# Small tiles of a key selection: flip, count and level moved from SBUF to a PSUM bank

## The chip, the cores and the metric

The kernel runs on one core of one Trainium2 chip. The metric is the device time of one execution in microseconds. A core has TensorE (PE, matrix products), VectorE (DVE), ScalarE (ACT), GpSimd (POOL) and SyncE (SP, which issues the DMAs). SBUF is the working memory on the chip. PSUM holds what TensorE writes, in banks of 2 KB per partition; VectorE and ScalarE can read and write it too.

## The reference

One inference step of two layers over a prompt of 1024 tokens and 64 sample tokens (8 sequences of 8), width 1024. Layer 0 is attention with sparse heads and dilated window heads behind one input projection; layer 1 is a recurrent block; each has an MLP behind it. What matters here is the start of layer 0:

```
h = einsum('btd,de->bte', rmsnorm(x), w_in)          # queries, keys, values, index queries, index keys, index weights
sc = sum over h of wi[q, h] * relu(qi[q, h] . ki[s])  # index scores, query by key
sc = where(key <= query, sc, NEG)
_, idx = top_k(sc, 256)                               # each query attends to its 256 best keys
```

The kernel needs no order of the 256 keys, only a mask of the chosen ones. For a row of scores it finds the 256th largest value bit by bit and then sets to NEG whatever lies below it. The outputs are the two activations, the new key/value rows and the recurrent states.

## The kernel before

The work runs in stages with a barrier of all engines between them: the projections with the key selection (stage_project), window attention, sparse attention, sample attention, output projection, MLP, recurrent block, MLP. The change touches the first stage alone.

**Projections.** The input projection is cut into eight groups of columns (`GROUPS`): kikv, qi, qa, qk0, qk1, qk2, v01 and v2, numbered 0 to 7. Each group is computed for nine tiles of tokens: tile 0 holds the 64 sample tokens, tiles 1 to 8 hold 128 prompt tokens each. A full tile of a group takes 24 matmuls (L845: eight slices of 128 input columns, each as high by high, high by low and low by high part); tile 0 takes 16. Tile p writes PSUM bank p % 3 and waits until ScalarE has copied tile p - 3 out (L775, into `rows`). The copied rows are squared on ScalarE (L797), summed per head and scaled on VectorE (L1024, L1029), rooted on ScalarE (L720), inverted and applied on VectorE one tile later (L1036, L1040), multiplied by the gains on GpSimd (L652) and stored by SP (L549). `rows` has three buffers, so a copy also waits for the store of the tile three before it. Tile 0 of a group needs an addition on GpSimd (L645) before it is squared.

**Weights.** SP loads a group's weights in eight parts into three buffers. VectorE casts a part to its high half (L993) and GpSimd subtracts to make the low half (L617). `WEIGHTS_AT` spreads the parts of group g + 1 over the tiles of group g - 1 and g (two tiles per three parts, beginning on the last tile of the group before). The parts stand first in VectorE's step, except on the last tile of a group, where they stand behind the normalisation.

**Selection.** Six tiles of prompt queries (2 to 7, rows of 384 to 1024 scores) need a selection; the scores lie in SBUF as `select_work`. It runs beside groups 2 to 7, tile by tile (`STEPS`, 54 of them), in 32 rounds y = 0 to 31, one for each bit of the bound:

- Two of the six (`OWN_TILES`) are tried by VectorE itself: `try_own` counts the scores at or above the bound with two instructions (L250), `move_own` turns the sign of the count into a bit (L269) and puts it into the bound (L271). The rounds are spread over 43 steps. In a step they stand around the normalisation: `try_own`, norms, `move_own`.
- The other four are tried by ScalarE: `show` runs four activations of 640 to 1024 scores with Sign and an accumulated sum of signs (L292), into `signs`. It waits (`tried`) for the bound of the round before. On VectorE `turn` adds `level` to `signs` to give `count` (L303), makes the bit (L310) and puts it into `minus` (L312; round 0 has L307 in place of these two). Round y is shown in step 1 + 4y/3, behind that tile's copy, square and root, and turned first in the next step, behind that step's weight parts.

Each of these operations on counts and bounds covers 2 or 4 elements per partition. All their tiles (`count`, `flip`, `level`, `signs`, `bound`, `minus`) are in SBUF. After round 31 `settle` and then `close` (24 slices in all, four of them for each of the six query tiles; those of the two own tiles come before) turn the bounds into masks on VectorE (L322 to L359). The stage ends when all engines are through; the first matmul of the window stage is L1657.

**The bank.** `psx` (turn_ps) is a PSUM bank of 512 columns, used for sums of squares, transposes of keys and queries and the mixed sample scores. Its last use in this stage is VectorE's copy of the sample scores to `sample_work`, ahead of `topk_sample()` and of the selection's rounds.

Of the kernel before, what the change touches and what calls it, by code (L numbers as in the profile page):

```python
# [10 lines left out]
I32 = mybir.dt.int32  # L11
ALU = mybir.AluOpType
# [4 lines left out]
P = 128  # L17
# [104 lines left out]
NSEL = len(SEL_TILES)  # L122
# [3 lines left out]
OWN_TILES = 2  # L126
# [73 lines left out]
class Handover:  # L200


    def __init__(self, nc, ctx):
        self.all = ctx.enter_context(nc.sbuf_tensor("unit_raw", [P, 2, KD * P], F32))
        self.flat = self.all[:, :, :].rearrange("p u n -> p (u n)")
        self.rows = self.flat[:, 0:2 * 3 * BW].rearrange("p (s n) -> p s n", s=2)
        self.rows_in = [ctx.enter_context(nc.semaphore(f"sw_first_in{i}")) for i in range(2)]
        self.unit_in = [ctx.enter_context(nc.semaphore(f"d_w_in{i}")) for i in range(2)]


class Select:
# [4 lines left out]
    def __init__(self, nc, ctx, work):  # L216
        def sb(name, shape, dt=F32):
            return ctx.enter_context(nc.sbuf_tensor("select_" + name, shape, dt))

        def sem(name):  # L220
            return ctx.enter_context(nc.semaphore("select_" + name))

        self.nc, self.work = nc, work
        self.junk = self.tied = self.shown = None
        self.count = sb("count", [P, NSEL])
        self.room = sb("room", [P, NSEL])
        self.flip = sb("flip", [P, NSEL], I32)
        self.bound = sb("bound", [P, NSEL], I32)
        self.signs = sb("signs", [P, NSEL - OWN_TILES])
        self.level = sb("level", [P, NSEL - OWN_TILES])  # L230
        self.minus = sb("minus_bound", [P, NSEL - OWN_TILES], I32)
        self.keep = sb("keep", [P, NSEL - OWN_TILES])
        self.done, self.ready, self.signed, self.tried = (sem(n) for n in ("done", "ready", "signed", "tried"))
        self.n = self.closed = 0
# [24 lines left out]
    def move_own(self, dve, y):  # L259

        nc = self.nc
        part = slice(0, OWN_TILES)
        dve.wait_ge(self.done, self.n)
        said = self.count[:, part].bitcast(I32)
        if y == 0:
            self.mark(nc.vector.tensor_scalar(self.bound[:, part], said, 31, 1 << 30, ALU.arith_shift_right, ALU.bitwise_xor))
        else:
            b = BITS - y
            self.mark(nc.vector.tensor_scalar(self.flip[:, part], said, 31, b, ALU.logical_shift_right, ALU.logical_shift_left))  # L269
            dve.wait_ge(self.done, self.n)  # L270
            self.mark(nc.vector.scalar_tensor_tensor(out=self.bound[:, part], in0=self.flip[:, part], scalar=1 << (b - 1) if b else 0,  # L271
                                                     in1=self.bound[:, part], op0=ALU.bitwise_xor, op1=ALU.bitwise_xor))

    def prepare(self, pool):
# [9 lines left out]
    def show(self, act, y):  # L284

        act.wait_ge(self.tried, self.PREPARED + y)
        for x in range(OWN_TILES, NSEL):
            c = x - OWN_TILES
            v = self.scores(x)
            if y or c:  # L290
                act.wait_ge(self.signed, (NSEL - OWN_TILES) * y + c)
            self.nc.scalar.activation(self.shown[:, 0:v.shape[1]], v, ACT.Sign, bias=self.minus[:, c:c + 1].bitcast(F32),  # L292
                                      accum_out=self.signs[:, c:c + 1]).then_inc(self.signed, 1)

    def turn(self, dve, y):

        nc = self.nc
        part = slice(OWN_TILES, NSEL)
        dve.wait_ge(self.signed, (NSEL - OWN_TILES) * (y + 1))
        dve.wait_ge(self.tried, self.PREPARED + y)  # L300
        if y:
            dve.wait_ge(self.done, self.n)
        self.mark(nc.vector.tensor_tensor(self.count[:, part], self.signs[:, :], self.level[:, :], ALU.add))  # L303
        dve.wait_ge(self.done, self.n)
        said = self.count[:, part].bitcast(I32)
        if y == 0:
            nc.vector.tensor_scalar(self.minus[:, :], said, 31, -(1 << 30), ALU.arith_shift_right, ALU.bitwise_xor).then_inc(self.tried, 1)  # L307
            return
        b = BITS - y
        self.mark(nc.vector.tensor_scalar(self.flip[:, part], said, 31, b, ALU.logical_shift_right, ALU.logical_shift_left))  # L310
        dve.wait_ge(self.done, self.n)
        nc.vector.scalar_tensor_tensor(out=self.minus[:, :], in0=self.flip[:, part], scalar=1 << (b - 1) if b else 0,  # L312
                                       in1=self.minus[:, :], op0=ALU.bitwise_xor, op1=ALU.bitwise_xor).then_inc(self.tried, 1)

    def settle(self, dve):
# [47 lines left out]
def stage_project(nc, a, xh, xl, rstd, ident, work, sel, proj, kiwi, smask, table, halves, strips, wstrips, hand):  # L363
# [7 lines left out]
    with ExitStack() as ctx:  # L371
# [50 lines left out]
        psx = ctx.enter_context(nc.psum_tensor("turn_ps", [P, 512], F32))  # L422
# [405 lines left out]
        def _(pe):  # L828
# [56 lines left out]
            def project_with_scores(gi, i, j, turn):  # L885
                for pair in range(IH // 2):
                    score_pair(j, pair)
                    if pair == 2 and turn is not None:
                        turn_queries(turn)
                    project(gi, i, pair, IH // 2)  # L890
# [87 lines left out]
        def _(dve):  # L978
            tk = [0]

            def link(ins):

                tk[0] += 1
                ins.then_inc(S["topk"], 1)
                dve.wait_ge(S["topk"], tk[0])
# [56 lines left out]
            def topk_sample():  # L1042
                for r in range(SR):
                    link(nc.vector.max(m8[0:TS, :], wks[:, 0:SKEYS]))
                    link(nc.vector.match_replace(wks[:, 0:SKEYS], m8[0:TS, :], wks[:, 0:SKEYS], SENT))
                if SREST:
                    link(nc.vector.max(m8[0:TS, :], wks[:, :]))
                    link(nc.vector.match_replace(wks[:, :], m8[0:TS, :], wks[:, :], SENT))
                link(nc.vector.tensor_scalar(wks[:, 0:SKEYS], wks[:, 0:SKEYS], SENT, NEG, ALU.not_equal, ALU.mult))
# [47 lines left out]
            nc.vector.tensor_tensor(wks[:, PAST:SKEYS], wks[:, PAST:SKEYS], after[:, :], ALU.add).then_inc(S["s_taken"], 1)  # L1097
            dve.wait_ge(S["s_taken"], 2)
            topk_sample()

            before, r0 = None, 0
            parts = [("own", y) for y in range(BITS + 1)] + [("close", x, z) for x in range(OWN_TILES) for z in range(sel.SLICES)]
# [740 lines left out]
def stage_sample(nc, a, ident, work, smp, proj, obp, mixed, oas, obs, own, hand):  # L1843
# [6 lines left out]
    with ExitStack() as ctx:  # L1850
# [189 lines left out]
        def _(pe):  # L2040
# [7 lines left out]
            def turn_group(g):  # L2048
                turn(2 + g, [768 * (g + 1) + P * i for i in range(4)])
# [1451 lines left out]
```

## Time and profile before

| | us |
|---|---|
| three runs | 2664.79, 2650.52, 2659.28; median 2659.28 |
| profiled execution, its own time | 2656.01 |
| its span, first to last instruction | 2653.1 |
| TensorE busy over the span | 2542.2 (96%) |
| VectorE, ScalarE, GpSimd busy | 1567.5, 1049.5, 1242.8 |
| mean granted clock of TensorE, as a share | 0.976 |

The rows further down come from the one profiled execution. Times in them are microseconds from the start of the span; "L310" is line 310 of the kernel. A duration that is longer than the same instruction takes elsewhere holds time in which the instruction was started and could not proceed.

### The profile page before, as it was taken

To read this page: it belongs to the slowest core of one execution; us is meant where nothing else is said; L and a number is where in the kernel's file an instruction comes from. 1 tells how busy PE (TensorE), PEld (TensorE's weight loads), DVE (VectorE), ACT (ScalarE), POOL (GpSimd) and SP (SyncE) were. 2 spreads that over 40 slices of the span, in tenths; PEclk is the share of its full clock that TensorE was granted. 3 is DMA by queue.
4 is the path that set the end of the run, shared out by engine and by line. 5 is a ranking of instruction groups with operands and counts; after the bars stand their busy time and mean duration, and the time that the engine had idled before them with its cause. 6 is when DMAs were issued, how large, how long until landed. Compare 5 with 4: busy or idle time off the path is not lost.

```text
span 2653.1 us, 44709 instructions
## 1 busy us (share of the span) xinstructions
PE 2542.2 (96%) x16674; PEld 2354.5 (89%) x16674; DVE 1567.5 (59%) x2510; ACT 1049.5 (40%) x1883; POOL 1242.8 (47%) x833
## 2 busy tenths in 40 slices
PE   7899999889879999999999989998999999999998
PEld 6567778766659999999999979998999999999998
DVE  6269897436555555545655687566355545554557
ACT  5347785766532322232233242535232233223322
POOL 4114441007436555555466573323355466545655
PEclk9989999889989999999999999999999999999999
DMA  5402222634371111111111112223111111111112
GB/s 149 135 24 72 78 80 87 214 99 133 106 259 62 40 52 50 34 47 55 42 45 47 48 32 69 88 112 141 42 40 56 40 40 55 47 40 47 55 48 84
DMA packets 109203, 198.71 MB, mean 75 GB/s; under 512 B 22709, under 2 KB 62773, under 8 KB 108805
## 3 DMA queue, kind: packets, MB, share of 16 engines
q1 hardware_dynamic: 104602, 191.85, 22.9%
q10 hardware_dynamic: 4480, 5.27, 0.6%
q8 instruction: 73, 1.20, 0.2%
q14 instruction: 48, 0.39, 0.0%
HBM read 170.97 MB, written 47.17 MB: 82 GB/s over the span
## 4 chain that ended last, share of the span: by engine, by line
PE 66%; DVE 3%; issue 1%; ACT 1%; POOL 0%; DMA 0%; DVEq 0%; ACTq 0%
PE d_ps L2348 40%; PE d_ps L2875 24%; PE d_ps L3237 1%; PE d_ps L2363 1%; DVE rstd_all L2435 0%; DVE x_t L2979 0%; DVE x_t L2970 0%; DVE xg_low L3365 0%; DVE xg_low L2374 0%; DVE m_hidden L2923 0%; PE d_ps L2408 0%; DVE m_shared_part L2970 0%; DVE unit_high L2331 0%; POOL unit_low L2335 0%; DMA mixed_low<-mixed_t 0%
## 5 line engine op out<-in xcount | busy, mean ns | idle before, releaser
L2348 PE MATMUL d_ps<-xg_high,unit_high 128*128 128x364 f32 (+1 forms) x2112 | 472.0, 332 | 8.1 <-DVE xg_low L3365 2.1
L2348 PE MATMUL d_ps<-xg_high,unit_low 128*128 128x364 f32 (+1 forms) x2112 | 464.7, 329 | 0.0
L2348 PE MATMUL d_ps<-xg_low,unit_high 128*128 128x364 f32 (+1 forms) x2112 | 464.3, 328 | 0.0
L2335 POOL TENSOR_TENSOR unit_low<-unit_raw,unit_high 128x1024 fp32r<-128x1024 f32 x96 | 232.5, 2422 | 410.6 <-DVE unit_high L2331 229.5
L2875 PE MATMUL d_ps<-m_hidden_high,unit_high 128*128 128x272 f32 x1792 | 374.8, 291 | 14.0 <-DVE x_t L2970 8.9
L2348 PEld LDWEIGHTS d_ps<-xg_high,unit_high 128*128 128x128 f32 x2112 | 365.1, 188 | 14.5 <-issue 5.5
L2875 PE MATMUL d_ps<-m_hidden_high,unit_low 128*128 128x272 f32 x1792 | 371.9, 289 | 0.0
L2875 PE MATMUL d_ps<-m_hidden_low,unit_high 128*128 128x272 f32 x1792 | 371.6, 289 | 0.0
L2348 PEld LDWEIGHTS d_ps<-xg_high,unit_low 128*128 128x128 f32 x2112 | 366.7, 189 | 0.0
L2348 PEld LDWEIGHTS d_ps<-xg_low,unit_high 128*128 128x128 f32 x2112 | 365.0, 188 | 0.0
L2725 POOL TENSOR_TENSOR unit_low<-unit_raw,unit_high 128x512 fp32r<-128x512 f32 x128 | 176.5, 1379 | 392.3 <-ACT unit_high L2793 390.9
L2970 DVE TENSOR_TENSOR x_t<-x_t,d_ps 128x544 f32<-128x544 f32 x320 | 227.4, 718 | 134.7 <-PE d_ps L2875 134.2
L2793 ACT ACTIVATE unit_high<-unit_raw 128x512 fp32r<-128x512 f32 x128 | 81.1, 634 | 568.8 <-PE d_ps L2875 353.6
L2875 PEld LDWEIGHTS d_ps<-m_hidden_high,unit_high 128*128 128x128 f32 x1792 | 282.4, 189 | 15.6 <-issue 15.4
L2875 PEld LDWEIGHTS d_ps<-m_hidden_high,unit_low 128*128 128x128 f32 x1792 | 284.4, 190 | 0.0
L2875 PEld LDWEIGHTS d_ps<-m_hidden_low,unit_high 128*128 128x128 f32 x1792 | 281.5, 189 | 0.0
L2718 POOL TENSOR_TENSOR m_hidden_low<-m_hidden,m_hidden_high 128x544 fp32r<-128x544 f32 x160 | 250.8, 1591 | 23.1 <-ACT m_hidden_high L2782 23.1
L2923 DVE SCALAR_TENSOR_TENSOR m_hidden<-d_ps,rstd_all 128x1092 f32<-128x1092 f32 x64 | 82.5, 1292 | 293.8 <-PE d_ps L2348 293.7
L845 PE MATMUL proj_ps<-w_high,x_high 128*128 128x512 f32 (+2 forms) x464 | 181.4, 391 | 10.8 <-ACT rows L775 10.7
L845 PE MATMUL proj_ps<-w_low,x_high 128*128 128x512 f32 (+2 forms) x464 | 176.8, 381 | 0.0
L845 PE MATMUL proj_ps<-w_high,x_low 128*128 128x512 f32 (+2 forms) x464 | 176.8, 381 | 0.0
L2787 ACT ACTIVATE unit_high<-unit_raw 128x1024 fp32r<-128x1024 f32 x60 | 63.6, 1060 | 250.5 <-PE d_ps L2875 127.2
(401 smaller groups left out, 4188.6 us busy)
## 6 DMA issues: line engine op xcount, KB each, us to landing
unit_raw<-w_units SPq DMA_DIRECT2D x160, 512.0 KB, 3.6
unit_raw<-w_in SPq DMA_DIRECT2D x48, 256.0 KB, 2.9
proj_rows<-rows SPq DMA_DIRECT2D x32, 256.0 KB, 2.0
s_win<-win_cache SPq DMA_DIRECT2D x2, 3968.0 KB
proj_rows<-rows SPq DMA_DIRECT2D x36, 128.0 KB, 1.8
sw_rows<-proj_rows SPq DMA_DIRECT2D x12, 384.0 KB, 5.2
select_work<-xt SPq DMA_DIRECT2D x8, 546.0 KB, 4.0
x_t<-xt SPq DMA_DIRECT2D x4, 1092.0 KB, 14.2
```

Of the source, the lines that this page charges most:

```text
L845: last = nc.tensor.matmul(ps[p % 3][:, 0:w], x, y[gi % 2][:, k, 0:w], start=(n == 0), stop=(n == len(passes) - 1))
L2335: self.nc.gpsimd.tensor_tensor(self.wl[slot][:, :], self.raw[:, slot, :], self.wh[slot][:, :].bitcast(F32), ALU.subtract).then_inc(self.w_ ...
L2348: last = self.nc.tensor.matmul(ps[:, c, 0:USED[c]], w[wslot][:, wk], v[:, k, c, 0:USED[c]], start=(k == 0 and n == 0), stop=(k == nk - 1 a ...
L2363: last = self.nc.tensor.matmul(ps[:, c, 0:USED[c]], w[wslot][:, wk], v[:, k, c, 0:USED[c]], start=(k == 0 and n == 0), stop=(k == nk - 1 a ...
L2718: nc.gpsimd.tensor_tensor(hl[:, i, q, :], SOURCES[i], hh[:, i, q, :].bitcast(F32), ALU.subtract).then_inc(h_low, 1)
L2725: nc.gpsimd.tensor_tensor(out, src, top.bitcast(F32), ALU.subtract).then_inc(part_low, 1)
L2787: nc.scalar.activation(d.wh[slot], d.raw[:, slot, :], ACT.Copy).then_inc(d.w_high, 1)
L2793: nc.scalar.activation(part_slots(d.high, x), src, ACT.Copy).then_inc(part_high, 1)
L2875: last = nc.tensor.matmul(out[:, c, :], w[:, i // 4, c0:c0 + P], h[:, i, q, HC * c:HC * (c + 1)], start=(i < 4 and q == 0 and x == 0), sto ...
L2923: nc.vector.scalar_tensor_tensor(out=v[:, t, :].rearrange("p (c n) -> p c n", c=NCH), in0=d.ps[t][:, :, 0:CH], scalar=0.0, in1=d.rstd[:, : ...
L2970: nc.vector.tensor_tensor(out, out, d.quarter[i], ALU.add).then_inc(added, 1)
L3237: last = nc.tensor.matmul(ps[use % 2][:, c, 0:CC], gw[:, n % 2, x, :], cv[:, n % 2, c, :], start=True, stop=True)
```

## The change

`flip` goes from SBUF to the bank `psx`: columns 0 to 1 for the own tiles, 2 to 5 for the four others. In `turn`, `count` (columns 8 to 11) and `level` (columns 12 to 15) are in the bank too. A new function `place`, called once ahead of the rounds, copies `level` there. `signs`, `minus`, `bound` and the own tiles' `count` stay in SBUF, and `settle` and `close` are as they were. `turn` now waits for `done` in round 0 as well. The SBUF tile `flip` is gone.

```diff
@@ Select.__init__
-        self.junk = self.tied = self.shown = None
+        self.junk = self.tied = self.shown = self.bank = None
-        self.flip = sb("flip", [P, NSEL], I32)
@@ move_own
             b = BITS - y
-            self.mark(nc.vector.tensor_scalar(self.flip[:, part], said, 31, b, ALU.logical_shift_right, ALU.logical_shift_left))
+            flip = self.bank[:, 0:OWN_TILES].bitcast(I32)
+            self.mark(nc.vector.tensor_scalar(flip, said, 31, b, ALU.logical_shift_right, ALU.logical_shift_left))
             dve.wait_ge(self.done, self.n)
-            self.mark(nc.vector.scalar_tensor_tensor(out=self.bound[:, part], in0=self.flip[:, part], scalar=1 << (b - 1) if b else 0,
+            self.mark(nc.vector.scalar_tensor_tensor(out=self.bound[:, part], in0=flip, scalar=1 << (b - 1) if b else 0,
                                                      in1=self.bound[:, part], op0=ALU.bitwise_xor, op1=ALU.bitwise_xor))
@@ new, ahead of turn
+    def place(self, dve, bank):
+
+        self.bank = bank
+        dve.wait_ge(self.tried, self.PREPARED)
+        self.mark(self.nc.vector.tensor_copy(bank[:, 2 * NSEL:2 * NSEL + NSEL - OWN_TILES], self.level[:, :]))
+
@@ turn
-        part = slice(OWN_TILES, NSEL)
+        level = self.bank[:, 2 * NSEL:2 * NSEL + NSEL - OWN_TILES]
+        count, flip = self.bank[:, NSEL + OWN_TILES:2 * NSEL], self.bank[:, OWN_TILES:NSEL].bitcast(I32)
         dve.wait_ge(self.signed, (NSEL - OWN_TILES) * (y + 1))
         dve.wait_ge(self.tried, self.PREPARED + y)
-        if y:
-            dve.wait_ge(self.done, self.n)
-        self.mark(nc.vector.tensor_tensor(self.count[:, part], self.signs[:, :], self.level[:, :], ALU.add))
         dve.wait_ge(self.done, self.n)
-        said = self.count[:, part].bitcast(I32)
+        self.mark(nc.vector.tensor_tensor(count, self.signs[:, :], level, ALU.add))
+        dve.wait_ge(self.done, self.n)
+        said = count.bitcast(I32)
...
-        self.mark(nc.vector.tensor_scalar(self.flip[:, part], said, 31, b, ALU.logical_shift_right, ALU.logical_shift_left))
+        self.mark(nc.vector.tensor_scalar(flip, said, 31, b, ALU.logical_shift_right, ALU.logical_shift_left))
         dve.wait_ge(self.done, self.n)
-        nc.vector.scalar_tensor_tensor(out=self.minus[:, :], in0=self.flip[:, part], scalar=1 << (b - 1) if b else 0,
+        nc.vector.scalar_tensor_tensor(out=self.minus[:, :], in0=flip, scalar=1 << (b - 1) if b else 0,
                                        in1=self.minus[:, :], op0=ALU.bitwise_xor, op1=ALU.bitwise_xor).then_inc(self.tried, 1)
@@ stage_project, vector
             topk_sample()
+            sel.place(dve, psx)
```

## Rows read from the trace of the kernel before

**Rows 1.** Engines by stretch: us, busy (instructions) per engine, PE clock, DMA share, GB/s.
```profile
203.00:437.00 234.00, 224.20 (x947) 177.85 (x946) 197.96 (x507) 190.52 (x372) 101.85 (x104) 0.99 0.25 80
400.00:437.00 37.00, 37.00 (x160) 29.80 (x159) 19.92 (x48) 31.29 (x60) 10.90 (x13) 1.00 0.29 91
...
927.00:2649.00 1722.00, 1697.26 (x11355) 1677.91 (x11353) 1000.70 (x1144) 533.14 (x707) 908.69 (x578) 1.00 0.17 56
```

**Rows 2.** Waits from 203 to 437 us: engine line, waited for: us, times, longest.
```profile
PE proj_ps L845 <- ACT rows L775: 9.8, 9, 2.0
...
ACT late L292 <- DVE select_minus_bound L312: 18.6, 13, 3.1
ACT head_roots L720 <- DVE head_means L1029: 11.2, 4, 9.1
ACT rows L775 <- DMA proj_rows<-rows: 8.3, 7, 2.5
ACT rows_sq L797 <- POOL rows L645: 7.2, 3, 3.6
```

**Rows 3.** VectorE groups, 203 to 437 us: count | busy us, mean ns | idle before.
```profile
L271 DVE SCALAR_TENSOR_TENSOR select_bound<-select_flip,select_bound 128x2 int32<-128x2 int32 x31 | 26.6, 857 | 1.1
...
L310 DVE TENSOR_SCALAR select_flip<-select_count 128x4 int32<-128x4 int32 x31 | 18.6, 602 | 1.1
...
L303 DVE TENSOR_TENSOR select_count<-select_signs,select_level 128x4 f32<-128x4 f32 x32 | 11.7, 364 | 24.1 <-ACT late L292 23.4
...
L269 DVE TENSOR_SCALAR select_flip<-select_count 128x2 int32<-128x2 int32 x31 | 7.2, 232 | 0.0
...
L312 DVE SCALAR_TENSOR_TENSOR select_minus_bound<-select_flip,select_minus_bound 128x4 int32<-128x4 int32 x30 | 5.9, 198 | 1.0
```

**Rows 4.** Single instructions, VectorE, in time order: start us, duration us, what.
```profile
214.20 1.29 DVE L310 TENSOR_SCALAR select_flip<-select_count 128x4 int32<-128x4 int32 x1
...
436.89 0.17 DVE L310 TENSOR_SCALAR select_flip<-select_count 128x4 int32<-128x4 int32 x1
```

**Rows 5.** The same for GpSimd, from 214 to 219 us.
```profile
214.17 1.29 POOL L617 TENSOR_TENSOR w_low<-unit_raw,w_high 128x512 fp32r<-128x512 f32 x1 [0.43 <-DVE w_high L993]
218.72 1.29 POOL L652 TENSOR_TENSOR rows<-rows,unit_raw 128x512 f32<-128x512 f32 x1 [3.26 <-DVE rows L1040]
```

**Rows 6.** VectorE again, 217.9 to 220 us, behind a normalisation.
```profile
217.95 0.69 DVE L1040 TENSOR_TENSOR rows<-rows,head_inverse 128x512 f32<-128x512 f32 x1
...
218.76 1.27 DVE L271 SCALAR_TENSOR_TENSOR select_bound<-select_flip,select_bound 128x2 int32<-128x2 int32 x1
219.95 0.42 DVE L993 CAST w_high<-unit_raw 128x512 fp32r<-128x512 f32 x1
```

**Rows 7.** Single lines over the span: count: ns min/median/max, first to last start.
```profile
L2970 DVE TENSOR_TENSOR x_t<-x_t,d_ps x320: 705/721/723, 927.4 to 2648.9; 128x544 f32<-128x544 f32 x160
...
L2374 DVE SCALAR_TENSOR_TENSOR xg_low<-x_t,params,xg_high x24: 1342/2466/3652, 794.2 to 1925.4; 128x1092 fp32r<-128x1092 f32 x24
...
L1066 DVE TENSOR_SCALAR mean_squares<-turn_ps x1: 172/172/172, 36.4 to 36.4; 128x9 f32<-128x9 f32 x1
```

**Rows 8.** The last show and the end of the stage, instructions in time order.
```profile
428.19 0.40 PE L845 MATMUL proj_ps<-w_high,x_low 128*128 128x512 f32 x1
...
431.50 0.67 ACT L775 ACTIVATE rows<-proj_ps,rstd_rows 128x512 f32<-128x512 f32 x1
...
436.70 0.16 DVE L303 TENSOR_TENSOR select_count<-select_signs,select_level 128x4 f32<-128x4 f32 x1 [3.37 <-ACT late L292]
...
464.56 0.47 ACT L775 ACTIVATE rows<-proj_ps,rstd_rows 128x256 f32<-128x256 f32 x1 [2.38 <-PE proj_ps L845]
...
465.42 0.45 SPq L604 DMA_DIRECT2D sample_mask<-sample_work  x1
...
469.52 0.69 DVE L359 TENSOR_SCALAR select_work<-late 128x1024 f32<-128x1024 f32 x1
...
470.54 1.09 PE L1657 MATMUL sw_ps_x<-ident,unit_raw 128*128 128x128 f32 x4 [6.01 <-PEq L371]
```

## The prediction

> **What bounds the kernel now.** I read the page first (TensorE is busy for 96% of the span), then the table of stretches, the waits and groups of the selection's stretch, and single instructions in time order. Only the first stage is touched, so all of the answer lies between the first show and the first matmul of the window stage.
>
> [rows 1] The stretch from 203 to 437 us holds the 32 rounds. TensorE issues 947 matmuls there in 234 us. In the undisturbed part, 400 to 437, it issues 160 in 37 us, one per 0.231 us. At that pace 947 take 219.0 us, so 15.0 us are lost. [rows 2] Of these 9.8 us are nine waits of TensorE for ScalarE's copy of a tile into `rows`; the other 5.2 are slower matmuls: 0.01 of the clock is missing over the stretch (0.99), some 2.3 us, and the first matmuls behind a wait. So TensorE has the most work of all and still waits: ScalarE runs behind it, and three PSUM banks let it lag only so far.
>
> ScalarE is busy for 190.5 of the 234 us, VectorE for 198.0 [rows 1]. Neither is the bound by its work. They hand the selection to each other: a show needs the bound from `turn`, `turn` needs the four sums. ScalarE waits 18.6 us in 13 waits for L312, the last instruction of `turn`; the other waits are those for the store of an older tile (8.3 us), for GpSimd's sum of a group's tile 0 (7.2 us) and for the head means (11.2 us, of which 9.1 are one wait that is over as the rounds begin) [rows 2].
>
> The end of the stage is not TensorE's either [rows 8]. Its last tile is copied out at 464.56, SP issues its last DMA at 465.42, but VectorE ends at 469.52 + 0.69 = 470.21, and the next stage's first matmul starts at 470.54. From the last `turn` (436.70) to 470.21 VectorE works through settle and close in 33.5 us that wait for no other engine. So the end follows the time of the last show, and that follows ScalarE, which starts to copy the tile of that show at 431.50, 2.9 us behind the end of its last matmul (428.19 + 0.40 = 428.59).
>
> **Where VectorE's time goes.** The instructions of `turn` and `move_own` touch 2 or 4 elements. Undisturbed, L310 takes 0.17 us; another took 1.29 us [rows 4]. That one started at 214.20, just behind GpSimd's L617 (214.17, 1.29 us long), and ended 0.03 us behind it [rows 5]. L271 the same: 218.76 to 220.03, beside GpSimd's L652, 218.72 to 220.01 [rows 5, 6]. So these small instructions are held until GpSimd's is through. In numbers [rows 3], taking 0.165 us for an undisturbed one (between L303's 0.16 in rows 8 and L310's 0.17 in rows 4): L310 18.6 - 31 x 0.17 = 13.3 us held; L303 11.7 - 32 x 0.165 = 6.4; L312 5.9 - 30 x 0.165 = 1.0; L271 26.6 - 31 x 0.165 = 21.5; L269 7.2 - 31 x 0.165 = 2.1. Together 44.3 us, of which 20.7 are in `turn`, with ScalarE waiting behind it.
>
> **The change, part by part.**
>
> *What holds an instruction.* L2970 adds a PSUM operand to an SBUF one. Its 320 instances last 705 to 723 ns [rows 7], in a stretch in which GpSimd is busy for 908.7 of 1722 us [rows 1]: many began while GpSimd was at work, and none was held. L2374 is a SCALAR_TENSOR_TENSOR with its tensors in SBUF: 1342 to 3652 ns for one shape [rows 7]. So what counts is where the operands lie. After the change every one of the five has at least one operand in PSUM and at most one input in SBUF, as L2970. I take all 44.3 us as gone from these lines. L303, L271 and L312 have the pattern of L2970 (one input each side). For L310 (PSUM to PSUM) and L269 (SBUF to PSUM) the trace has nothing that writes to PSUM from VectorE; between all held as now (13.3 + 2.1 us kept) and none, I take none, as the two nearest rows, L2970 and L1066, show no hold. If they stay held, `turn` keeps 13.3 of its 20.7 us.
>
> *The price of a small PSUM access.* L1066 reads 9 elements from this very bank in 0.172 us [rows 7], against 0.17 for 4 elements in SBUF. So 0 us each; bounds: -0.05 us (a write to PSUM might end sooner), and +0.52 us, if each took the 0.69 us of an SBUF instruction on 512 elements such as L1040 [rows 6]. The nearest row is L1066. There are 32 x 3 + 31 x 2 = 158 of them. The Trainium skill speaks against the change here: "VectorE: DVE Perf Modes", section "The TRN2 errata — SBUF-src ops pay a fixed extra latency per instruction", gives VectorE a fixed 58 cycles from SBUF and 120 from PSUM at 0.96 GHz, 0.065 us more for each. By that rule `turn` would be 0.19 us longer in each of 32 rounds, an estimate of 6 us on the loop between ScalarE and VectorE, and the sum below would be smaller by up to 2 us, since TensorE covers most of it. L1066 does not show it.
>
> *`place`.* One copy of 4 elements, 0.17 us, bounds 0 and 0.7, ahead of round 0, on VectorE. GpSimd set `level` long before. It stands in front of the first weight parts and the first `try_own`; the first turn (idle in front of L303 adds up to 24.1 us in all [rows 3]) takes it up. Cost 0. The wait that `turn` gains in round 0 is for an instruction of VectorE's own queue: 0.
>
> *What comes late next.* Behind `move_own` VectorE often has a weight cast (L993), with both operands in SBUF. Today L271 waits out GpSimd's gain multiplication and the cast finds the way free (219.95, 0.42 us) [rows 6]. With L271 short, the cast arrives 1.1 us sooner, while L652 still runs, and is held in its place. Five of nine tiles of a group begin with a cast, and one more has it in front of `move_own`. So of L271's 21.5 us I give back two thirds, 14; what VectorE really gains is 44.3 - 14 = 30 us, and 198.0 becomes 168, 51 us below TensorE's 219. `turn` keeps all it gains: its instructions stand behind the cast, whose L617 on GpSimd is what holds them now.
>
> *What it does to ScalarE.* `turn` gives 20.7 us over 32 rounds; ScalarE waits for it in 13 of them, 18.6 us. Waits are worst where the turn is held (the 3.1 us are about three instructions of 1.2). I take 12 of the 18.6 as gone directly, and a part of the 8.3 for stores, since normalisation on VectorE gets through sooner too. The 7.2 for tile 0 stay: they are GpSimd's order. ScalarE's waits sum to 45.3 us in the rows, which with its busy 190.5 is more than 234: that of 9.1 us began before the stretch. Without it 36.2 are left, and 190.5 + 36.2 leaves 7 us for gaps between instructions. Less 14 us, ScalarE is through in 220, as fast as TensorE's 219. ScalarE's lag then shrinks instead of reaching the three banks' limit.
>
> *The sum.* Of the 15.0 us that TensorE loses it gets back 12; 3 I leave for the starts of groups, where tile 0 still makes ScalarE wait. Of the 2.9 us that ScalarE lags at the last show 2 go. The last turn then comes 14 us sooner, at 422.7, VectorE ends at 456.2. TensorE's side ends 12 us sooner: the last copy at 452.6, SP's last DMA at 453.4, so the barrier stays VectorE's. The later stages move as a block. Profiled execution: 2656.0 - 14 = 2642.0; the median of the runs stands 3.3 above it, so 2659.3 - 14 = **2645.3 us**.
>
> **The rivals.**
>
> *Half of it.* The hold moves on to the casts and to L1040, stores and tile 0 make ScalarE wait again as soon as `turn` doesn't. For it: L271's hold does move, and the waits not for `turn` sum to 26.7 us. Against it: these are counted with lags that come from `turn` itself. Only the directly held share, 12 of 18.6, works on TensorE's 9.8: 6.3 us, plus 1 at the end: 7 us, 2652.3 us.
>
> *The waits just change names.* ScalarE comes earlier and waits for the store of the tile three before it. Against it: 8.3 us stand there now, against 18.6. Gain 2 us, 2657.3 us.
>
> *Slower.* PSUM accesses of small size cost. One mechanism: each of the 158 instructions pays x more on VectorE. It decides from 44.3 / 158 = 0.28 us each. At the bound of 0.52 us, 82 us come against the 44.3, VectorE is at 198.0 + 38 = 236 us, over the stretch's 234, and each turn is 3 x 0.52 - 20.7 / 32 = 0.9 us longer. In the 13 rounds in which ScalarE waits now it all goes on to ScalarE and, with its lag at the limit, to TensorE: 12 us, 2671 us. L1066 speaks against it; nothing here shows a write.
>
> *It does not free them.* A hold stays since `signs`, `minus` and `bound` are in SBUF. L2970, with x_t in SBUF, speaks against it. Time 2659; I count it with the second rival.
>
> **How the numbers follow.** The forecast 0.66; half 0.22; changed names or not freed 0.07; slower 0.05. The likeliest case's own range is a gain of 10 to 17.9 (15.0 + 2.9, all of both), 2641 to 2649. About 0.5%, 13.3 us, is what a measurement of this kernel can tell from no change. Within the forecast, as a triangle from 10 over 14 to 17.9, two thirds lie above 13.3: faster 0.66 x 2/3 = 0.44, slower 0.05, the rest 0.51. The range reaches from 2640 (all of both, with 1 us for the runs' spread) to 2657 (the second rival).
>
> **What would show it.** Right: L303, L310, L312, L269 and L271 each at 0.15 to 0.2 us without exception; casts (L993) with more of 1 us and above; TensorE's waits for L775 under 3 us; the last turn near 423; the window stage's first matmul near 456.5; all later stages of the same length. Wrong: L310 with rows of 1.2 us (writes to PSUM are held), small instructions above 0.25 us (PSUM costs), or short ones with ScalarE's waits as large as now under other names. If VectorE ends before SP, the last part of the sum fails, and the end is TensorE's.

## The result, and the profile after

The changed kernel takes 2640.47 us (median of 6 runs, 2633.17 to 2644.54) beside 2660.09 us for the kernel before (6 runs). The ratio is 0.9926, 95% interval [0.9904, 0.9948]: faster, by 14 to 26 us. The forecast was 2645.3 us, in a range from 2640.0 to 2657.0, so the measured median lies 0.5 us above the range's lower end. The profiled execution took 2638.77 us with a span of 2635.9, against 2656.01 and 2653.1: 17.2 us less, where the sum had said 14.

First the stretch with the rounds in the changed kernel, with the columns of [rows 1].

```profile
203.00:437.00 234.00, 234.00 (x1059) 191.65 (x1059) 178.18 (x540) 192.71 (x378) 102.80 (x105) 1.00 0.26 84
```

TensorE is busy for all of the 234 us at a granted clock of 1.00; before it lost 15.0. (It issues 1059 matmuls, since the short ones of the last group now begin inside the stretch.) Its waits for `rows` are gone from the list. ScalarE's waits, with the columns of [rows 2]:

```profile
ACT rows L781 <- PE proj_ps L851: 18.2, 9, 4.9
...
ACT rows_sq L803 <- POOL rows L651: 6.8, 3, 3.8
ACT rows L781 <- DMA proj_rows<-rows: 4.7, 4, 1.9
ACT late L292 <- DVE select_minus_bound L318: 2.2, 2, 1.5
```

The wait for `turn` fell from 18.6 us to 2.2, and ScalarE now waits for TensorE: the order of the two is turned round. The 7.2 us for tile 0 (now 6.8) stayed, but cost nothing: TensorE has no wait for ScalarE in the stretch, so ScalarE never falls so far behind that a bank is missing.

VectorE's groups, to be read beside [rows 3] (L309 was L303, L316 was L310, L318 was L312, L999 was L993; L271 and L269 kept their numbers):

```profile
L999 DVE CAST w_high<-unit_raw 128x512 fp32r<-128x512 f32 x28 | 21.9, 788 | 7.2 <-DMA unit_raw<-w_in 7.2
...
L316 DVE TENSOR_SCALAR turn_ps<-turn_ps 128x4 int32<-128x4 int32 x31 | 5.3, 170 | 1.1
L309 DVE TENSOR_TENSOR turn_ps<-select_signs,turn_ps 128x4 f32<-128x4 f32 x32 | 5.2, 163 | 35.5 <-ACT late L292 35.3
...
L318 DVE SCALAR_TENSOR_TENSOR select_minus_bound<-turn_ps,select_minus_bound 128x4 int32<-128x4 int32 x31 | 5.0, 161 | 1.1
L271 DVE SCALAR_TENSOR_TENSOR select_bound<-turn_ps,select_bound 128x2 int32<-128x2 int32 x31 | 4.9, 159 | 1.1
L269 DVE TENSOR_SCALAR turn_ps<-select_count 128x2 int32<-128x2 int32 x31 | 4.8, 155 | 0.0
```

and, from the kernel before, the casts:

```profile
L993 DVE CAST w_high<-unit_raw 128x512 fp32r<-128x512 f32 x28 | 15.9, 584 | 0.4 <-DMA unit_raw<-w_in 0.4
```

None of the five is held in any round; the longest single one of them takes 171 ns. The casts, with their operands in SBUF, took over 6.0 us of it. L1046, the normalisation (L1040 before), is 0.9 us longer (27.2 to 28.1) and L1035, the head means (L1029 before), 1.3 us (9.3 to 10.6). From the first show to the end of the last turn VectorE is busy for 161.0 us, where it was 197.5.

The end of the stage, beside [rows 8], instructions in time order:

```profile
413.54 0.39 PE L851 MATMUL proj_ps<-w_high,x_low 128*128 128x512 f32 x1
...
413.97 0.69 ACT L781 ACTIVATE rows<-proj_ps,rstd_rows 128x512 f32<-128x512 f32 x1 [0.56 <-PE proj_ps L851]
...
419.00 0.17 DVE L309 TENSOR_TENSOR turn_ps<-select_signs,turn_ps 128x4 f32<-128x4 f32 x1 [3.88 <-ACT late L292]
...
449.90 0.47 ACT L781 ACTIVATE rows<-proj_ps,rstd_rows 128x256 f32<-128x256 f32 x1 [2.38 <-PE proj_ps L851]
...
450.76 0.45 SPq L610 DMA_DIRECT2D sample_mask<-sample_work  x1
451.68 0.69 DVE L365 TENSOR_SCALAR select_work<-late 128x1024 f32<-128x1024 f32 x1
...
453.21 0.63 PE L1664 MATMUL sw_ps_x<-ident,unit_raw 128*128 128x128 f32 x4 [3.35 <-PEq L377]
```

The tile of the last show ends at 413.93 and is copied at 413.97: the lag of 2.9 us is 0.04. The last turn is 17.7 us sooner, TensorE's last copied tile 14.7, the window stage's first matmul 17.3. The gap between TensorE's two stages shrank from 6.0 to 3.35 us.

What ends the stage has changed hands. In the kernel before, SP's last DMA (the sample mask) had landed at 467.4, and VectorE ended 2.8 us after it, at 470.21. In the changed kernel VectorE ends at 452.37 (17.8 us sooner), and the same DMA, issued behind the last store at 450.76, lands 2.0 us later, at 452.76: 0.4 us after VectorE. At the barrier behind it (L371, now L377) SP waits 2.8 us for the others in the kernel before and 0.2 us in the changed one. The time of the DMA (KB, us from issue to landing) is the same in both:

```profile
sample_mask<-sample_work SPq DMA_DIRECT2D x1, 66.0 KB, 2.0
```

From the window stage on the two traces have the same length: 470.54 to 2653.1 is 2182.6 us, 453.21 to 2635.9 is 2182.7.

### The profile page after: what moved, and what is told of

Its sections match the earlier page's. It is cut to its first block, busy times and chain, and to the rows that moved or that the text cites. A ratio compares the mean times of both kernels' runs of the same rounds, so it can differ in the third digit from the quotient of the medians.

```text
span 2635.9 us, 44711 instructions
## 1 busy us (share of the span) xinstructions
PE 2535.3 (96%) x16674; PEld 2352.2 (89%) x16674; DVE 1528.4 (58%) x2511; ACT 1048.3 (40%) x1883; POOL 1243.2 (47%) x833
## 4 chain that ended last, share of the span: by engine, by line
PE 66%; DVE 3%; issue 1%; ACT 1%; POOL 0%; DMA 0%; DVEq 0%; ACTq 0%; POOLq 0%
PE d_ps L2355 40%; PE d_ps L2882 24%; PE d_ps L3244 1%; PE d_ps L2370 1%; DVE rstd_all L2442 0%; DVE xg_low L3372 0%; DVE x_t L2977 0%; DVE xg_low L2381 0%; DVE x_t L2986 0%; DVE m_hidden L2930 0%; PE d_ps L2415 0%; DVE m_shared_part L2977 0%; DVE unit_high L2338 0%; POOL unit_low L2342 0%; DMA mixed_low<-mixed_t 0%
```

## The experiments

The time of a whole run swings: the six of the kernel before reach from 2650.5 to 2664.8 us, the six of the changed one from 2633.2 to 2644.5. Part of the swing lies ahead of the selection: the first show of the changed kernel is at 203.6 us in one profile and at 199.8 in another. So each experiment has, beside its ratio, the length L from the first show (L292's first start) to the window stage's first matmul in its one profile. It is 267.0 us in the kernel before (203.56 to 470.54) and 249.6 in the changed one (203.59 to 453.21); the others come from starts rounded to 0.1 us. The first show is read from a line such as this, of the kernel before (ns min/median/max, first to last start):

```profile
L292 ACT ACTIVATE late<-select_work,select_minus_bound x128: 814/992/1157, 203.6 to 435.4; 128x640 f32<-128x640 f32 x32, 128x768 f32<-128x768 f32 x32, 128x896 f32<-128x896 f32 x32, 128x1024 f32<-128x1024 f32 x32
```

| kernel | L, us | against before | ratio, 95% interval |
|---|---|---|---|
| before | 267.0 | | |
| changed, first profile | 249.6 | -17.4 | 0.9926 [0.9904, 0.9948] |
| r_after | 249.1 | -17.9 | 0.9911 [0.9895, 0.9927] |
| e1_turn_only | 250.6 | -16.4 | 0.9935 [0.9917, 0.9953] |
| e2_own_only | 262.8 | -4.2 | 0.9973 [0.9960, 0.9986] |
| e3_turn_flip_sbuf | 250.3 | -16.7 | 0.9938 [0.9918, 0.9959] |
| e4_no_gains | 249.1 | -17.9 | 0.9944 [0.9924, 0.9963] |
| e5_delay3 | 254.3 | -12.7 | 0.9942 [0.9921, 0.9964] |
| e6_delay12 | 309.0 | +42.0 | 1.0138 [1.0116, 1.0161] |
| e7_sooner | 250.6 | -16.4 | 0.9941 [0.9924, 0.9957] |
| e8_behind_cast | 259.7 | -7.3 | 0.9965 [0.9949, 0.9980] |
| e9_elsewhere | 259.2 | -7.8 | 0.9964 [0.9947, 0.9980] |

Which engine ends the stage differs too. In r_after, e1 and e4 it is, as in the changed kernel, SP's last DMA, which lands 0.3 to 0.4 us after VectorE's end; in e3 the two fall together. In e2, e5, e6, e8 and e9 it is VectorE again, 2.6, 3.1, 9.1, 4.4 and 4.2 us after the DMA has landed.

**r_after**, the changed kernel again.

> The changed kernel again, beside the others of this call. The profiled run of it was 17.2 us shorter than that of the kernel before, the medians 19.6 us apart. Theory (the stage up to the window stage is all of it): 17 to 18 us, ratio 0.9933, and the window stage's first matmul at 453 us. Rival (some 2 us more come from elsewhere, as the medians say): ratio 0.9925 or below, with a later stage shorter than in the kernel before.

L repeats to 0.5 us. The ratio does not come out as 0.9933: its interval begins at 0.9895 and ends at 0.9927. The rival's second condition does not hold either: neither profile has a later part that is shorter than in the kernel before (here 448.9 to 2637.0, 2188.1 us, is even longer). So 17 to 18 us are shown in the stage, and what the medians have beyond that (19.6 us apart in one comparison, 22.5 in the other, so 2 and 5 us more) stays open.

**e1_turn_only** and **e2_own_only** take the change apart.

```diff
 e1: move_own
-            flip = self.bank[:, 0:OWN_TILES].bitcast(I32)
+            flip = self.flip[:, part]
 ... (and the SBUF tile flip is back)
```

> Only turn works in the bank; the own tiles' flip is in SBUF again. Theory (what counts is turn's 20.7 us of holds, for which ScalarE waits; those of move_own have slack): L271 is held again, 27 us busy for 31, and yet the gain stays at 13 to 16 of 17 us. Rival (VectorE's load counts, whichever line carries it): half of the holds stay, so half of the gain, 8 to 9 us.

```diff
 e2: the kernel before, move_own
-            self.mark(nc.vector.tensor_scalar(self.flip[:, part], said, ...
+            flip = self.bank[:, 0:OWN_TILES].bitcast(I32)
+            self.mark(nc.vector.tensor_scalar(flip, said, ...
 ... (the next instruction reads this flip, and psx is made the bank ahead of the rounds)
```

> Only the own tiles' flip is in the bank; turn is as in the kernel before. Theory: L271 falls to 0.16 us each, about a third of its 21.5 us goes on to the weight casts, L310 and L303 stay held (19 us together), and the gain is 2 to 5 us. Rival (load): 8 to 9 us, as much as with turn alone.

With `turn` alone in the bank the second instruction of `move_own` (now L272) is held in every round, and 16.4 of the 17.4 us are there:

```profile
L272 DVE SCALAR_TENSOR_TENSOR select_bound<-select_flip,select_bound x31: 654/724/1284, 211.6 to 380.5; 128x2 int32<-128x2 int32 x31
```

With the own flip alone it is free, and TensorE still waits for 6.9 us (L293, L313, L776 and L846 were L292, L312, L775 and L845):

```profile
L272 DVE SCALAR_TENSOR_TENSOR select_bound<-turn_ps,select_bound x31: 158/159/160, 208.2 to 388.9; 128x2 int32<-128x2 int32 x31
```
```profile
ACT late L293 <- DVE select_minus_bound L313: 14.8, 10, 3.2
...
PE proj_ps L846 <- ACT rows L776: 6.9, 8, 1.9
```

Holds of nearly the same sum (20.7 us in `turn`, 23.6 in `move_own`) are worth 16.4 us in one place and 4.2 in the other. Not all of that is place: in e2 the casts take 9.6 us more than in the kernel before (27.6 instead of 18.0, both widths), in e1 they take none, so VectorE's busy time from the first show to the last turn falls by 12.8 us in e2 and by 20.1 in e1. For each microsecond off VectorE the stage still gains 0.33 us in e2 and 0.82 in e1. VectorE's load as such was not it. e2's gain is in the range given for the theory; e1's is 0.4 us above it.

**e3_turn_flip_sbuf** asks which operands count.

```diff
-        count, flip = self.bank[:, NSEL + OWN_TILES:2 * NSEL], self.bank[:, OWN_TILES:NSEL].bitcast(I32)
+        count, flip = self.bank[:, NSEL + OWN_TILES:2 * NSEL], self.flip[:, OWN_TILES:NSEL]
 ... (and the SBUF tile flip is back)
```

> As the changed kernel, but turn's flip is in SBUF: count and level are in the bank, so the instruction that makes the bit reads PSUM and writes SBUF, and the next one has two inputs in SBUF (flip and minus). Theory (an instruction is held when GpSimd is at work and both inputs are in SBUF, or one input and the output): L303's and L310's successors take 0.17 us, but the third is reached 0.4 us after the cast while GpSimd's 1.3 us subtraction still runs, and is held for up to 1 us in the rounds behind a cast: 10 to 14 us on it in all, and the gain is 7 to 12 us. Rival (reading PSUM anywhere in the chain is enough): no holds, gain as the changed kernel, 17 us.

```profile
L319 DVE SCALAR_TENSOR_TENSOR select_minus_bound<-select_flip,select_minus_bound x31: 161/247/1101, 213.6 to 419.9; 128x4 int32<-128x4 int32 x31
```

The mechanism is as the theory said: the one instruction of `turn` that has two SBUF inputs left is held, up to 1101 ns and 13.5 us busy in all, while the one that reads PSUM and writes SBUF goes free (161 to 165 ns). What it costs was not: ScalarE waits 6.2 us for it, TensorE 0.4 us, and the stage loses 0.7 us instead of 5 to 10, less than the theory and more than the rival, which had no hold at all. So 8.4 us of holds (13.5 less 31 undisturbed ones) are nearly covered.

**e4_no_gains** asks who holds L271. GpSimd multiplies 2 elements of each tile by the gains instead of all; the rest goes without.

```diff
-                    nc.gpsimd.tensor_tensor(v, v, gains[:, row:row + 1, :].broadcast_to([P, hn, HD]),
+                    nc.gpsimd.tensor_tensor(v[:, 0:1, 0:2], v[:, 0:1, 0:2], gains[:, row:row + 1, 0:2],
```

> The kernel before, with GpSimd's multiplication by the head gains cut to 2 elements of each tile (the gains of the rest are left out). L652 then takes under 0.3 us instead of 0.7 to 1.3. Theory (it is L652 that holds L271, and L617 that holds turn's instructions): L271 falls from 26.6 us to 5 to 7 us for 31, L303 and L310 keep 25 to 32 us together, and the stage from the first show to the first matmul of the window stage takes 258 to 264 us, against 267.0 before and 262.8 with only the own flip in the bank. Rival (any GpSimd instruction, however short, or the instruction's own form makes L271 0.65 us and more): L271 stays at 0.65 us or above.

```profile
L271 DVE SCALAR_TENSOR_TENSOR select_bound<-select_flip,select_bound x31: 160/171/1270, 207.8 to 373.3; 128x2 int32<-128x2 int32 x31
```
```profile
L310 DVE TENSOR_SCALAR select_flip<-select_count x31: 169/170/1295, 210.0 to 414.8; 128x4 int32<-128x4 int32 x31
```

L652 was what held L271: with operands in SBUF as before its median is 171 ns instead of 720, and its one long instance (1270 ns) ends with another GpSimd instruction, the addition L645. L310 is still held, up to 1295 ns, but less often, and here the theory fell short. It had the holds in `turn` stay; yet from 203 to 437 us L310 took 13.5 us instead of 18.6 and L303 7.7 instead of 11.7, 21.2 together where 25 to 32 were expected. So with L652 short half of `turn`'s holds went as well (10.6 us are left of 20.7). In the trace each held instruction can be matched with the GpSimd instruction that ends just before it. In the kernel before 30 of the 31 held L271 belong to L652; in `turn` L652 held L303 in 8 rounds (2.7 us), and all the rest is L617's, 13 rounds of L310 among them. In e4 L617 meets L310 in 8 rounds instead of 13. So most of what went from `turn` are meetings with L617 that no longer happen once GpSimd and VectorE run at other times. ScalarE's wait for `turn` fell to 6.8 us, TensorE's for ScalarE to nothing, and the stage took 249.1 us instead of 258 to 264. The stage can be freed from GpSimd's side as well, here in a kernel that leaves the gains out.

**e5, e6, e8, e9** put time into `turn` with no GpSimd in it. To the changed kernel each adds instructions of 4 elements from the bank to the bank, some 0.2 us apart. e8 and e9 give them to different rounds: e8 to those whose turn stands behind a weight cast, e9 to the others.

```diff
+        for _ in range(3):                 # e6: 12; e8: 6 behind a cast, else 0; e9: 7 where no cast is ahead, else 0
+            self.mark(nc.vector.tensor_scalar(self.bank[:, 16:20].bitcast(I32), said, 31, 1, ...
+            dve.wait_ge(self.done, self.n)
```

> The changed kernel with 3 more instructions of 4 elements, bank to bank, in each turn of rounds 1 to 31: 0.6 us a round, 19 us in all, about what the holds in turn were (20.7 us), but spread evenly and without GpSimd. Theory (the old cost came from lumps of 1.2 to 3.2 us in the rounds behind a cast, on top of a late VectorE; even delays are covered, since ScalarE waits 18 us for TensorE in the changed kernel): the stage from first show to window takes 249.5 to 252 us, against 249.6 and 249.1. Rival (19 us between show and show cost the same however they are spread): 260 to 263 us, as with only the own flip in the bank.

> The same with 12 more instructions: 2.4 us a round, 76 us in all, 63 us of them busy. VectorE's 178 us busy in 234 become 241, so it is the bound. Theory: the cover ends between 0.6 and 2.4 us a round; the stage takes 259 to 270 us, TensorE waits for the copies again, 8 us and more. Rival (only ScalarE's chain counts: copy, square and root cover 1.4 us of a turn, and the tile without a show one whole turn in four tiles): 250 to 255 us.

> The changed kernel with 6 more instructions of 4 elements, bank to bank, in the turns that stand behind a weight cast alone (17 of 31 rounds): 1.2 us each, 20 us in all, without GpSimd's part in it. This is the holds' size and place. Even, the same 19 us took the stage from 249.6 to 254.2 us; as holds (only the own flip in the bank) from 249.6 to 262.8. Theory (size and place decide, since VectorE comes late to just these turns): 259 to 263 us. Rival (the holds cost more because GpSimd and the casts are in them too, not by their place): 253 to 256 us.

> The same with 7 more instructions in the other 14 turns, those without a cast ahead: 1.4 us each, 19.6 us in all. Theory (place decides: these rounds have VectorE idle when the sums come): 250 to 254 us. Rival (only the size of a lump counts): as with the lumps behind the casts, 259 to 263 us.

| | added in a turn | added in all | L longer than 249.6 by | share of it |
|---|---|---|---|---|
| e5 | 0.6 us in 31 rounds | 19 us | 4.7 us | 0.25 |
| e8 | 1.2 us in 17 rounds | 20 us | 10.1 us | 0.50 |
| e9 | 1.4 us in 14 rounds | 20 us | 9.6 us | 0.49 |
| e6 | 2.4 us in 31 rounds | 74 us | 59.4 us | 0.80 |

e5 lies between its theory (249.5 to 252 us, it took 254.3) and its rival; e6 missed both its ranges (259 to 270, and 250 to 255) by far; e8 is in its theory's range and e9 in its rival's. The rounds behind a cast are no worse than the others: the theory of the place fell with e9, and the size of a lump decides. Part of a turn is covered, since ScalarE has the next tile's copy, square and root to do meanwhile (0.68, 0.63 and 0.19 us, 1.5 in all). Beyond the cover it is paid in full: from e5 to e6 55 us are added and L grows by 54.7. In e5, e8 and e9 TensorE waits for ScalarE for 1.5, 3.8 and 3.9 us; the rest of the loss is at the end, where the last turn, and with it VectorE's end, comes later.

It is not VectorE's load either, 234 of 287 us in e6:

```profile
203.00:490.00 287.00, 254.61 (x1081) 202.22 (x1080) 234.04 (x903) 195.26 (x379) 101.64 (x105) 0.95 0.23 71
```

but the hand-over round by round: in these 287 us ScalarE waits 47.5 us for `turn`, TensorE 32.3 us for ScalarE, and the mean granted clock is 0.95, where it was 0.99 in the kernel before. Against the changed kernel, e2's holds in `turn` (22.5 us) cost 13.2 us, e8's delay (20 us, behind the casts) 10.1. e2's holds are 2 us more and its casts take 3.2 us longer than the changed kernel's; how much of the 3 us between the two comes from that is not shown.

**e7_sooner** tries for more.

```diff
-        SHOW_AT = {STEPS[1 + 4 * y // 3]: y for y in range(BITS + 1)}
+        SHOW_AT = {STEPS[1 + 5 * y // 4]: y for y in range(BITS + 1)}
+                if (gi, i) == (NGR - 1, 0):            # moved here from behind the last store
+                    sp.wait_ge(S["topk"], 2 * SR + 2 * (SREST > 0) + 1)
+                    sp.dma_start(smask, wks[:, 0:SKEYS]).then_inc(S["mask_out"], 16)
 ...
```

> The changed kernel with round y shown at tile 1 + 5y/4 instead of 1 + 4y/3 (last show at tile 40 of 54 instead of 42, counted from 0: 39 and 42), and the DMA of the sample mask issued at the start of group v2 instead of behind the last store. Theory (the end is now VectorE's by 0.5 us over TensorE's and SP's): VectorE ends some 10 us sooner, and the next stage starts when the last store has landed: 0.3 to 1.0 us sooner than in the changed kernel, which no measurement can tell. Rival (four shows in five tiles are too many for ScalarE, 24.5 us of its work against TensorE's 27.9, with the waits at the starts of groups): TensorE waits for copies again, 2 to 6 us slower than the changed kernel.

L is 250.6 us, 1.0 longer than in the changed kernel: neither the theory's 0.3 to 1.0 shorter nor the rival's 2 to 6 longer. VectorE now ends at 445.38, 9.5 us before the window stage's first matmul (454.90), and the mask's DMA is long done, so only TensorE's own side is left: its last tile, the copy, the store and its landing. That side is not shorter: TensorE waits again for ScalarE, by 0.6 us. The change had already brought the stage down to that side, and nothing tried here went clearly below it.

## Why the prediction was right, and where it was small

- **What holds the small instructions: right.** All five went to means of 155 to 170 ns, those two without a row (writes to PSUM) among them. e3 shows the hold come back on the one instruction given two SBUF inputs, e4 shows it leave with GpSimd's work. In the kernel before each held instance of the five ends 0.02 to 0.07 us behind the end of a GpSimd L652, L617 or L645. The Trainium skill says so ("SBUF — State Buffer", section "Who interferes with whom": a VectorE instruction with two SBUF inputs contends with a GpSimd instruction that reads SBUF, and one in a two-port mode contends with GpSimd); the traces agree for two SBUF inputs, at up to 1101 ns against 161 for the same instruction in e3. L310, with one SBUF input and its output in SBUF, was held for up to 1.30 us; in what mode it ran no trace shows.
- **The price of a small PSUM access: right, 0.** L316, bank to bank, takes 0.170 us, as in SBUF; L269, SBUF to bank, 0.155. The 0.065 us more, an estimate from the fixed cycles in the Trainium skill's "VectorE: DVE Perf Modes", section "The TRN2 errata — SBUF-src ops pay a fixed extra latency per instruction", does not show at this size.
- **The hold moves on: right in kind, too large.** Given back were 14 us; the 128x512 casts took 6.0 (21.9 - 15.9), and L1046 and L1035, which the prediction did not have, 2.2. So VectorE gained 36.5 us, not 30. (The count of 158 instructions is one too many, since round 0 has two in `turn`, and L307's own hold of 1.0 us is missing from the 44.3; neither matters to the sum.)
- **`turn` counts, `move_own` little: right.** The sum gave the gain to ScalarE's waits, and e1 against e2 (16.4 against 4.2 us) shows it.
- **The sum: 14 instead of 17.3, by two terms.** "3 I leave for the starts of groups" was 0.3: tile 0's waits stayed at 6.8 us, but TensorE felt none of them, as ScalarE's lag stays within three banks, and TensorE's last tile is copied 14.7 us sooner. "Of the 2.9 us that ScalarE lags 2 go": all of it went, and VectorE's end came 17.8 us sooner, nearly the upper bound of 17.9.
- **"The barrier stays VectorE's": wrong, by 0.4 us.** The prediction set SP's last DMA by its issue and left out the 2.0 us until it lands. The 2.8 us by which VectorE ended behind that landing were used up, since VectorE gained 3.1 us more than TensorE's side (17.8 against 14.7). By the prediction's own sign (VectorE ends before SP) the last part of the sum fails. It cost 0.5 us: 17.3 instead of 17.8.
- **The range and the chances.** That the time is in the range is close: 2640.47 us against a lower end of 2640.0, which allowed for all of both terms and 1 us of spread. The repeat's median was 2638.76, below it, and the medians differ by 2 to 5 us more than the stage explains, a part that the sum did not have. The chance of 0.51 for a change within 0.5%, against 0.44 for more, leaned on the held-back 3 us; the interval lies around 0.74% faster.
- **Rivals.** "Half of it" and "changed names" are out: the gain is 17.3 us and not 7 or 2, and the waits for stores fell with the rest, from 8.3 to 4.7 us, where names would have had them grow. "It does not free them" is out with the five means, "slower" with the price of an access.

## What to carry to other kernels

Look at the longest duration of VectorE's tiniest instructions beside GpSimd's in the same microseconds: a row of 4 elements at 1.2 us is a wait that no list of waits shows. Where two engines hand work to each other in rounds, size the cure by the part of the hand-over that is not covered: here some 20 us of delay cost 10 us in lumps of 1.2 to 1.4 us, 4.7 us spread over all rounds, and off the chain, as the 23.6 us of holds of `move_own` in e1, 1.0 us. Where a bound on the gain is clean (what TensorE loses, plus the lag at the end), hold little of it back once the chain behind the loss falls below the bound's own load. And for each engine that ends a stage, note by how much the next one is ahead, with a DMA counted to its landing: that is how far the gain reaches before another end takes over.

## What was not expected of the hardware

A GpSimd instruction of 254 ns on average (e4's L652) hardly holds anybody, where the full one of 0.7 to 1.3 us held an instruction of 2 elements in all 31 rounds (never under 652 ns). The hold ends with GpSimd's instruction, 0.02 to 0.07 us behind it in the kernel before, so its length is what is left of that. A hold that is taken away goes in part to the next instruction with its operands in SBUF: the casts are 9.6 us longer in e2 and 6.4 in the changed kernel (both widths). A VectorE instruction of 2 or 4 elements of `turn` or `move_own` that is not held costs 147 to 171 ns with its operands in SBUF or in PSUM, as input or as output.
